# GpSimd makes the lower part of the last 512 columns of each full down slab in the light blocks

## What is computed

```python
def swiglu(x, w_gate, w_up, w_down):
    return (jax.nn.silu(x @ w_gate) * (x @ w_up)) @ w_down

def run(args):                      # one block of tokens, one expert e
    xb, e = args
    return swiglu(xb, w_gate[e], w_up[e], w_down[e])
```

## Time and profile before

| | before |
|---|---|
| median of 3 runs | 1376.87 us (1371.97 to 1378.08) |
| the profiled execution | 1381.79 us, of which the span of instructions is 1379.9 us |
| PE busy | 1321.5 us (96%) |
| DVE busy | 1142.8 us (83%) |
| ACT busy | 876.3 us (64%) |
| POOL busy | 81.3 us (6%), 64 instructions |
| LO subtractions, line 1158, x383 | 794.2 us on DVE |
| loads | 376.36 MB read from HBM |

### The profile page before, as it was taken

One profiled execution on the slowest core, in us unless ns is written; L12 is line 12 of the kernel. 1 busy time (PEld: TensorE's weight loads), 2 busy tenths in 40 slices (PEclk: granted clock), 3 DMA queues, 4 the chain that ended last, 5 costly groups with the idle time before them and its releaser, 6 DMA issues.

```text
span 1379.9 us, 17431 instructions
## 1 busy us (share of the span) xinstructions
PE 1321.5 (96%) x6156; PEld 990.4 (72%) x6156; DVE 1142.8 (83%) x1233; ACT 876.3 (64%) x964; POOL 81.3 (6%) x64
## 2 busy tenths in 40 slices
PE   5999999999999999999999999999999999999998
PEld 3887678888887887678666676666766667666676
DVE  5988967655447989875998988999889998899998
ACT  3344644544434445635776777987779877798775
POOL 0011010100000020010051000000000000000400
PEclk9999999999999999999999999999999999999999
DMA  7434333975483344242899999999999999999996
GB/s 288 183 140 159 129 127 132 339 296 182 169 343 122 152 152 163 81 176 92 316 358 372 416 358 377 393 400 421 393 354 411 402 422 382 363 408 402 420 393 252
DMA packets 63564, 394.67 MB, mean 286 GB/s; under 512 B 6914, under 2 KB 7486, under 8 KB 23818
## 3 DMA queue, kind: packets, MB, share of 16 engines
q1 hardware_dynamic: 58778, 375.37, 70.0%
q10 hardware_dynamic: 2848, 11.53, 2.1%
q0 software_dynamic: 1872, 6.91, 1.5%
HBM read 376.36 MB, written 17.43 MB: 285 GB/s over the span
## 4 chain that ended last, share of the span: by engine, by line
PE 70%; DVE 19%; issue 5%; ACT 4%; DMA 1%; POOL 0%; DVEq 0%; SPq 0%; ACTq 0%
PE bank L1726 15%; PE bank L1727 15%; DVE w_lo L1158 13%; PE bank L2025 13%; PE bank L2002 9%; PE bank L1776 5%; ACT w_hi L770 2%; PE bank L1871 2%; PE bank L1771 2%; PE bank L1739 1%; PE bank L1864 1%; PE bank L2012 1%; DVE ys L1147 1%; PE bank L1881 1%; DVE act L1538 1%
## 5 line engine op out<-in xcount | busy, mean ns | idle before, releaser
L1158 DVE TENSOR_TENSOR w_lo<-raw,w_hi 128x2048 fp32r<-128x2048 f32 (+2 forms) x383 | 794.2, 2089 | 95.2 <-ACT w_hi L770 93.8
L770 ACT ACTIVATE w_hi<-raw 128x2048 fp32r<-128x2048 f32 (+2 forms) x383 | 669.6, 1755 | 130.6 <-PE bank L2025 57.4
L1726 PE MATMUL bank<-w_hi,hT_hi 128*128 128x512 f32 (+3 forms) x968 | 386.3, 399 | 4.2 <-DVE hT_lo L1147 2.9
L1727 PE MATMUL bank<-w_hi,hT_lo 128*128 128x512 f32 (+3 forms) x968 | 378.2, 391 | 0.0
L1726 PEld LDWEIGHTS bank<-w_hi,hT_hi 128*128 128x128 f32 (+1 forms) x968 | 172.2, 178 | 54.3 <-issue 6.7
L1727 PEld LDWEIGHTS bank<-w_hi,hT_lo 128*128 128x128 f32 (+1 forms) x968 | 172.3, 178 | 45.4 <-issue 1.0
L2002 PE MATMUL bank<-w_lo,hT_hi 128*96 128x512 f32 (+3 forms) x616 | 162.4, 388 | 0.8 <-DVE w_lo L1158 0.8
L2002 PEld LDWEIGHTS bank<-w_lo,hT_hi 128*96 128x96 f32 (+1 forms) x616 | 103.1, 169 | 37.4 <-DVE w_lo L1158 4.3
L1776 PE MATMUL bank<-w_lo,hT_hi 128*128 128x512 f32 x352 | 87.4, 390 | 0.0
L2087 PE MATMUL bank<-w_lo,hT_hi 128*128 128x512 f32 (+1 forms) x264 | 78.2, 414 | 8.8 <-DVE w_lo L1158 8.7
L971 ACT ACTIVATE act_hi<-bank 128x192 fp32r<-128x192 f32 (+1 forms) x66 | 24.8, 376 | 95.2 <-PE bank L2012 95.2
(11 more groups left out here) (282 smaller groups left out, 1355.6 us busy)
## 6 DMA issues: line engine op xcount, KB each, us to landing
raw<-in_moe SPq DMA_DIRECT2D x240, 1024.0 KB, 7.9
raw<-in_mix SPq DMA_DIRECT2D x56, 1024.0 KB, 4.9
raw<-in_dense SPq DMA_DIRECT2D x30, 1024.0 KB, 4.9
raw<-in_moe SPq DMA_DIRECT2D x16, 768.0 KB, 8.5
raw<-in_moe SPq DMA_DIRECT2D x12, 512.0 KB, 7.2
slot_h<-x_squared ACTq DMA_DIRECT2D x1, 5632.0 KB, 42.0
slot_y<-x_squared ACTq DMA_DIRECT2D x1, 5632.0 KB, 24.3
raw<-in_moe SPq DMA_DIRECT2D x8, 256.0 KB, 4.7
```

The lines of the kernel that those rows point to most:

```text
L770: nc.scalar.activation(HI[:, split_slot, 0:width], RAW[:, raw_slot, half:half + width], ACT.Copy)\
L1158: vec.tensor_tensor(LO[:, split_slot, 0:width], RAW[:, raw_slot, half:half + width], HI[:, split_slot, 0:width].bitcast(F32), ALU.subtract ...
L1726: mm(out_, left[0], right[0], start=start, stop=False)
L1727: mm(out_, left[1], right[1], start=False, stop=False)
```

## The change

DVE makes LO only for columns 0 to 1535 of the ten full down slabs (p = 6, 9, ... 33) of blocks 2, 4 and 6. POOL makes columns 1536 to 2047, as soon as `hi_ready` has reached the slab, and counts them in a new semaphore `pool_lo_ready`. PE waits for this count before the fourth matmul of the LO pass, and SP waits for it before it loads into a buffer that held such a slab. The number of columns computed, the loads and the results are the same.

```diff
+LIGHT_BLOCKS = tuple(2 * i + 2 for i in range(LIGHT))
+LIGHT_DOWN = range(6, 34, 3)
+VECTOR_PART = SLAB - 512
     @block.sync
-        def put(slot, dst, src, free):
+        def put(slot, dst, src, free, pool_parts=None):
             if free is not None:
                 sp.wait_ge(lo_ready, free)
+            if pool_parts is not None:
+                sp.wait_ge(sem("pool_lo_ready"), pool_parts)
             sp.dma_start(dst, src).then_inc(raw_loaded[slot], 16)
     @block.gpsimd
+        for b in LIGHT_BLOCKS:
+            for p in LIGHT_DOWN:
+                n = FIRST["ffn", 1] + FFN_SLABS * b + p
+                raw, split = block_place(1, b, p) % RAW_SLOTS, (FIRST["ffn", 1] + p) % SPLIT_SLOTS
+                pool.wait_ge(hi_ready, n + 1)
+                nc.gpsimd.tensor_tensor(LO[:, split, VECTOR_PART:SLAB], RAW[:, raw, VECTOR_PART:SLAB],
+                                        HI[:, split, VECTOR_PART:SLAB].bitcast(F32), ALU.subtract).then_inc(sem("pool_lo_ready"), 1)
         pool.wait_ge(y_free, 16 * LIGHT + 32)
     @block.vector, light_block
-                ffn_split(6, b, n0)
+                ffn_split(6, b, n0, VECTOR_PART)
                     ffn_split(p + 4, b, n0, width)
                     turned_lo_light(q)
-                    ffn_split(p + 5, b, n0)
+                    ffn_split(p + 5, b, n0, VECTOR_PART)
     @block.tensor
             def down_light(n, s, q, start, tiles=(0, 1), amid=None, pool_parts=None):
                 for j, k in enumerate(tiles):
                     for half in range(2):
                         at = j * D + half * 512
+                        if at == VECTOR_PART and pool_parts is not None:
+                            pe.wait_ge(sem("pool_lo_ready"), pool_parts)
                         ins = mm(PS[4 + half][:, :], R["act_hi"][:, k, 0:2 * LCAP], LO[:, s, at:at + 512], start=False, stop=False)
```

More of the change, by code:

```diff
@@ L586, in _, with pool_parts_by @@
     def _(sp):
-        def put(slot, dst, src, free):
+        def put(slot, dst, src, free, pool_parts=None):
             if free is not None:
                 sp.wait_ge(lo_ready, free)
+            if pool_parts is not None:
+                sp.wait_ge(sem("pool_lo_ready"), pool_parts)
             sp.dma_start(dst, src).then_inc(raw_loaded[slot], 16)
+        def pool_parts_by(b, p, late=False):
+            before = p - back(p, late)
+            if not isinstance(b, int) or before % FFN_SLABS not in LIGHT_DOWN or b + before // FFN_SLABS not in LIGHT_BLOCKS:
+                return None
+            return NCH * LIGHT_BLOCKS.index(b + before // FFN_SLABS) + LIGHT_DOWN.index(before % FFN_SLABS) + 1
         sp.dma_start(IDENT[:, :], cst_d[:, 0:P]).then_inc(sem("ident_loaded"), 16)
@@ L607, in _, with two_halves, slab @@
             blocks = slabs["dense" if layer == 0 else "moe"]
-            def two_halves(e, b, p, n):
+            def two_halves(e, b, p, n, pool_parts=None):
                 slot, at = block_place(layer, b, p) % RAW_SLOTS, slice(SLAB_AT[p % FFN_SLABS], SLAB_AT[p % FFN_SLABS + 2])
                 put(slot, RAW[:, slot, :].rearrange("p (h n) -> p h n", h=2),
-                    blocks[e, at].rearrange("o (h p n) -> p (o h) n", h=2, p=P), n - back(p % FFN_SLABS) + 1)
-            def slab(e, b, p, n, late):
+                    blocks[e, at].rearrange("o (h p n) -> p (o h) n", h=2, p=P), n - back(p % FFN_SLABS) + 1, pool_parts)
+            def slab(e, b, p, n, late, pool_parts=None):
                 slot, at, width = block_place(layer, b, p, late) % RAW_SLOTS, slice(SLAB_AT[p], SLAB_AT[p + 1]), width_of(("ffn", layer), p)
@@ L621, in slab @@
                     put(slot, RAW[:, slot, cols], blocks[e, at].rearrange("o (p n) -> p (o n)", p=P)[:, cols],
-                        None if i else n - back(p, late) + 1)
+                        None if i else n - back(p, late) + 1, None if i else pool_parts)
             def block_slabs(n0, e, b, y_at=None, y_light_at=None, tok_at=None, tok_heavy_at=None):
@@ L627, in block_slabs @@
                 for p in (0, 2):
-                    two_halves(e, at, p, n0 + p)
+                    two_halves(e, at, p, n0 + p, pool_parts_by(b, p) if layer == 1 else None)
                 for i in range(4):
                     for j in range(6):
-                        slab(e, at, 4 + 6 * i + j, n0 + 6 * i + 4 + j, at == NE - 1 and 4 + 6 * i + j >= LATE_SLAB)
+                        part = 4 + 6 * i + j
+                        late = at == NE - 1 and part >= LATE_SLAB
+                        slab(e, at, part, n0 + part, late, pool_parts_by(b, part, late) if layer == 1 else None)
                     if i == 0 and (y_at or y_light_at):
@@ L643, in block_slabs @@
                         sp.dma_start(TOK_HEAVY[0:tok_heavy_at[1], :], slot_h[bass.ds(*tok_heavy_at), :]).then_inc(tok_heavy_loaded, 16)
-                    slab(e, at, p, n0 + p, at == NE - 1)
+                    slab(e, at, p, n0 + p, at == NE - 1, pool_parts_by(b, p, at == NE - 1) if layer == 1 else None)
             if layer == 0:
@@ L2102, in turn_act_light, with down_light @@
                 ins.then_inc(turned, 1)
-            def down_light(n, s, q, start, tiles=(0, 1), amid=None):
+            def down_light(n, s, q, start, tiles=(0, 1), amid=None, pool_parts=None):
                 pe.wait_ge(act_hi_ready, q + 1)
@@ L2145, in light_block, with pair @@
                     gate_up_light(n0 + part, slot(part), 2 * part, 2, CHUNK, 0)
-                def pair(n0, qb, k0, start):
+                def pair(n0, qb, k0, w0, start):
                     for j in range(2):
@@ L2157, in pair @@
                             pe.wait_ge(y_taken, 2 * b + 2)
-                        down_light(n0 + p + 2, slot(p + 2), q - 1, opening)
+                        down_light(n0 + p + 2, slot(p + 2), q - 1, opening, pool_parts=w0 + j + 1)
                         add_lo(k0 + 1 + j, 1 - j)
-                pair(n0, qb, k0, True)
+                pair(n0, qb, k0, NCH * l, True)
                 with pe.Fori(1, 4) as i:
-                    pair(pe.snap(6 * i + n0), pe.snap(2 * i + qb), pe.snap(2 * i + k0), False)
+                    pair(pe.snap(6 * i + n0), pe.snap(2 * i + qb), pe.snap(2 * i + k0), pe.snap(2 * i + NCH * l), False)
                 q = qb + NCH - 1
@@ L2167, in light_block @@
                 gate_up_light(n0 + 29, slot(29), 4, 4, CHUNK, 1)
[L2168 removed]
+                down_light(n0 + 30, slot(30), q - 1, False, pool_parts=NCH * l + NCH - 1)
                 add_lo(k0 + NCH - 1, 1)
@@ L2172, in light_block @@
                 gate_up_light(n0 + 32, slot(32), 4, 4, TAIL, 0)
-                down_light(n0 + 33, slot(33), q, False, amid=lambda: add_lo(k0 + NCH, 0, TAIL))
+                down_light(n0 + 33, slot(33), q, False, amid=lambda: add_lo(k0 + NCH, 0, TAIL),
+                           pool_parts=NCH * l + NCH)
                 turn_act_light(q + 1)
```

## The result

The changed kernel takes 1398.98 us (median of 3, 1398.8 to 1401.59) against 1376.87: a ratio of 1.0178, 95% interval 1.0155 to 1.0201, or +22.1 us. The forecast was +15.8 us (1392.7, range 1379 to 1403). The direction held, and so did the exclusion that it rests on. But more than half of the loss comes from a wait of PE that the sum had at nothing.

A forecast was written before the change was run, and what follows sets the result against it. DVE was taken to bound the light blocks, PE the heavy ones. Per light block 9 x 0.54 + 0.4 = 5.3 us, three blocks +15.8, so 1376.87 + 15.8 = 1392.7 us, range 1379 to 1403.

The forecast's parts named there:

- a wait of PE that the sum had at nothing: Ahead of the fourth LO matmul: POOL done at 894.58, before DVE's own part at 896.32, so nothing queues.
- What bounds the stage: Light blocks are DVE's, heavy blocks PE's; DVE is spared 0.53 us per down slab, at most 16.0 us over 30.
- POOL's time: One POOL subtraction of 128x512 from two SBUF inputs: 1.15 us taken, with 0.47 and 1.42 as ends.
- Mutual exclusion: POOL moves nothing while DVE's two-SBUF-input subtraction runs, and POOL's subtraction holds DVE likewise; rows showed only the first direction.
- A chunk with POOL first: Light-block chunk, POOL running before LO of down: +0.54 us, from 1.15 + 0.06 less 0.13 and 0.53.
- the grown chunk repeats itself: Nine of ten down slabs per light block keep the same order, HI ready about 1 us before the LO ahead ends.
- the first slabs: First down slab (p = 6) of each light block: small subtraction 0.4 us late, PE needs it, so +0.4 us each.
- SP's wait at nothing: Ahead of loads into such a buffer, SP already waits for DVE's later LO of the same slab: 0.
- the third rival: PE's longer rests in light blocks drop its clock once or twice more per block: +5 to +10 us, 1398 to 1403.
- The first rival: POOL doesn't hold DVE, LO of down starts at its old place; loads limit the gain: 1373 us, chance 0.12.
- The second: POOL is cheap (0.47 to 0.8 us), holding DVE about as long as spared: 1373 to 1383 us, chance 0.09.
- the signs that were listed: Light-block timeline: POOL at an LO's end, LO of down 1.1 us late, chunk 7.7 us, heavy blocks unchanged, loads under 8.6.

The follow-up runs named there:

- e1: Changed kernel without POOL's part and all waits for it; low part of the last 512 columns left out: 1370.91 us against 1373.87, ratio 0.9977.
- e2: Kernel before, DVE making all 2048 columns, plus POOL's 30 subtractions on other tiles, only SP waiting for them: 1439.13 us, ratio 1.0461.
- e10: Changed kernel, POOL also waiting for the end of DVE's LO of the slab before: 1411.48 us against 1373.36, ratio 1.0276.
- e5: Changed kernel, POOL's subtraction replaced by a 128x512 memset in a spare tile, same waits: 1372.41 us against 1373.87, ratio 0.9984.
- e9: Changed kernel, DVE waiting for its own previous subtraction before LO of down, except at a block's first: 1381.49 us against 1373.36, ratio 1.0062.
- e8: e2 with SP's wait for POOL's subtractions taken out too: 1392.77 us against 1373.36, ratio 1.0143.

## Why the prediction was right, and where it was off

**What bounds the stage**: right. DVE's relief alone gives 3.0 us (e1), and the two limits behind it, ACT at about 6.8 and the loads at about 7.4 us a chunk, came out of rows 4, 8 and 10. Busy time spared on the bounding engine (16 us) was no measure of the gain.

**POOL's time**: 1.15 us was taken between 0.94 and 1.42; it is 1.16 from the end of DVE's subtraction (880.90 to 882.06). The estimate of 1.12 us from the Trainium skill, GPSIMD Engine Reference, section 3.1, is near it. From start to end, with nobody in its way, the operation takes 1.26 to 1.31 (e2, e10).

**Mutual exclusion**: right, and shown from DVE's side by e2 (+0.91 in DVE's own subtractions) and bounded by e5 (a POOL operation that only writes isn't held, and holds nobody). This was the one thing that rows 5 couldn't give, and the prediction's direction rested on it.

**A chunk with POOL first**: forecast +0.54, measured +0.38. DVE's shortened subtraction ends 1.62 us after POOL, not 1.74, since part of its start passes while it is held up, and the handover is within the 1.16 us.

**The step that failed**: "the grown chunk repeats itself". I had POOL get in at the first end of a subtraction in all nine slabs of a block, and if not, behind LO of down, for "+0.68, the same within the range". It gets in at the first end in two of three. In the third it isn't one subtraction late but two, and by then PE is waiting for POOL, and the folding matmul, ACT's SiLU and DVE's multiplication with it, 2.35 us or more. I named what would queue behind PE if POOL were the later one, and priced it at nothing, for lack of a row with POOL refused twice. Those nine were worth 18.2 us, where the sum had 4.9 for them; the other 18 were worth 7.1, where it had 9.7; the first slabs 0, where it had 1.2.

So the number is in part luck. The mechanism that the sum was made of, every POOL in at the first end, is e9, and it costs +8.1 us, half of the forecast. The time came out within 1386 to 1401 because the late ones, which the sum didn't price, outweighed what it had too much.

**The other edits.** SP's wait at nothing: right here, but e2 shows that it holds only as long as somebody else stops DVE first. PE's clock, the third rival: in the changed kernel it falls to its lower level (1.2 GHz) behind some late chunks; the stage view of after, in the columns of the earlier trace rows:

```profile
868.00:874.00 6.00, 5.15 (x17) 4.08 (x18) 3.10 (x4) 2.97 (x4) 2.47 (x2) 0.72 0.83 320
```

PE had stood for over 2 us ahead of it. That late chunk and the one behind it take 17.28 us together, where 9.03 and 7.52 make 16.55. The clock falls so behind five of the nine, each time for 3.4 us, and costs 0.5 to 0.8 us each, some 3 us in all. The mean clock of the first light block went from 0.98 to 0.96. In e9, with no late chunk, 862 to 905 us are at 1.00. So the clock follows the late ones, and is a small part of what they cost. The 1398 to 1403 us of that rival hold the measured time, but not for its reason.

**The first rival** (no hold) is out by e2 and e9. Its price, -4 us, was near e1's -3.0. **The second** (POOL is cheap) is out by 1.16 us. Of the signs that were listed, POOL's place at the end of a subtraction, the heavy blocks and the loads issued at 900 to 906 us, which land after 6.7 us, not 8.6, were there, and the chunk is 7.52 us, not 7.7. Two signs of the hold were not. LO of down doesn't start 1.1 us late, it starts at its old place and lasts longer, and DVE's busy time hardly falls (1142.8 to 1142.2 us), with no idle time of DVE put down to POOL. By the test named for the first rival, LO of down at its old place, that rival would have been taken for true. The length of the operation and of the chunk decides, not its start. There was also the sign listed as a sign of the contrary, PE idle ahead of the fourth LO matmul with POOL as releaser. It didn't mean that the exclusion is missing, but that it goes on for longer.

## What to carry to other kernels

A subtraction of two SBUF tiles on GpSimd takes the place of VectorE's, it doesn't run beside it: before moving columns there, compare GpSimd's 2.2 ns a column with the 1.04 spared, not the idle time of GpSimd with VectorE's load. Look for the hold in the length of VectorE's operations, for no idle time shows it. If a small consumer on GpSimd can't be avoided, make sure that VectorE lets it in, with one wait on VectorE's own last subtraction: it was worth 14 of 22 us here. And before taking time off the bounding engine, run the stage with that work left out: it shows what the next limits leave of the gain.

## What was not expected of the hardware

- A GpSimd subtraction of 1.3 us can last 48.9 us (e8), refused while VectorE issues subtractions back to back, although VectorE's small operations with a PSUM operand lie between them.
- Whether GpSimd gets in hangs on VectorE's own waits: all nine late ones of the changed kernel followed a multiplication whose SiLU had been ready for 0.21 us or more, none of the other 18 did, and a wait of VectorE on its own counter (e9) brought the late ones to none. What in VectorE's issue makes that difference wasn't tried further and stays open.
- A GpSimd memset of 128x512 is 0.52 to 0.53 us long in all 30 cases beside VectorE's subtractions (e5).
